# Four of each eight tokens' gated first one-hots made on GpSimd with scalar operands, the other four compared on VectorE

## The reference

```python
q = (xb @ w_q).reshape(PEER_BLOCK, PEER_HEADS, 2, PEER_QDIM // 2)
s = jnp.einsum('thpd,hpkd->thpk', q, subkeys)
s1, i1 = lax.top_k(s[:, :, 0], PEER_TOPK)
s2, i2 = lax.top_k(s[:, :, 1], PEER_TOPK)
...
sc, pos = lax.top_k(cand, PEER_TOPK)
idx = jnp.take_along_axis(cidx, pos, axis=-1)
g = jax.nn.softmax(sc, axis=-1)
act = jax.nn.gelu(jnp.einsum('thkd,td->thk', u[idx], xb))
return jnp.einsum('thk,thkd->td', g * act, v[idx])
```

## Time and profile before

| what | value |
|---|---|
| device time, 3 runs | 3705.79, 3709.24, 3708.85 us; median 3708.85 us |
| span of the profiled execution, first to last instruction | 3700.4 us; no separate total is given for that execution |
| PE, DVE, ACT, POOL busy | 96%, 72%, 54%, 4% of the span |
| gate phases, about | 1084 to 1181, 1970 to 2061, 3252 to 3338 us |
| POOL multiplies of the gate phase | 96, 102 us in all |

### The profile page before, as it was taken

How to read it: one execution, slowest core, us unless ns; L and a number is a source line. 1 busy time by engine, 2 the same in 40 slices (tenths; PEclk the granted TensorE clock), 3 DMA queues, 4 the chain that set the end, 5 groups by cost and what they waited for, 6 DMA issues and landing times.

```text
span 3700.4 us, 61292 instructions
## 1 busy us (share of the span) xinstructions
PE 3558.4 (96%) x22710; PEld 3113.8 (84%) x22710; DVE 2666.9 (72%) x5607; ACT 2003.8 (54%) x3922; POOL 139.6 (4%) x134
## 2 busy tenths in 40 slices
PE   7999999999998999999999999999899999979999
PEld 5877787888887899999998888888698888878888
DVE  5447733699868688888767776774765899686666
ACT  3345522566668555555557544434454666684444
POOL 0002000000012000000002000000100000030000
PEclk9999999999999999999999999999999999999999
DMA  5213222455645566566655566633044566605665
GB/s 206 82 67 138 94 97 83 144 183 182 186 151 159 167 187 184 185 186 184 187 184 152 161 186 198 195 119 111 9 164 136 176 187 182 187 29 165 188 190 172
DMA packets 142313, 568.38 MB, mean 154 GB/s; under 512 B 15920, under 2 KB 17456, under 8 KB 130352
## 3 DMA queue, kind: packets, MB, share of 16 engines
q1 hardware_dynamic: 142128, 566.16, 49.0%
HBM read 565.05 MB, written 1.05 MB: 153 GB/s over the span
## 4 chain that ended last, share of the span: by engine, by line
PE 82%; DVE 12%; ACT 3%; issue 2%; DMA 1%; POOL 1%; SPq 0%; DVEq 0%; POOLq 0%; ACTq 0%
PE ps L584 52%; PE ps L1081 13%; PE ps L1099 10%; PE ps L1083 6%; DVE low L1835 3%; DVE arena L1835 3%; ACT arena L1283 2%; DMA ring<-wmod_in 1%; POOL arena L2619 1%; DVE hot_found L1835 1%; DVE arena L2387 1%; DVE arena L2378 1%; DVE ring_low L1835 0%; DVE arena L2380 0%; DVE arena L2375 0%
## 5 line engine op out<-in xcount | busy, mean ns | idle before, releaser
L1283 ACT ACTIVATE high<-ring 128x512 fp32r<-128x512 f32 x1632 | 1028.4, 632 | 1014.7 <-PE ps L584 502.2
L1835 DVE TENSOR_TENSOR low<-ring,high 128x512 fp32r<-128x512 f32 x1632 | 1078.1, 690 | 290.4 <-ACT high L1283 279.4
L584 PE MATMUL ps<-h_pair,high 128*128 128x512 f32 x3456 | 1236.7, 398 | 17.6 <-DVE h_pair L1835 10.3
L584 PE MATMUL ps<-h_pair,low 128*128 128x256 f32 x3456 | 979.7, 283 | 0.0
L584 PEld LDWEIGHTS ps<-h_pair,high 128*128 128x128 f32 x3456 | 653.6, 189 | 171.1 <-issue 11.9
L1081 PE MATMUL ps<-wt,high 128*128 128x512 f32 x2016 | 706.3, 397 | 5.7 <-DVE low L1835 5.7
L584 PEld LDWEIGHTS ps<-h_pair,low 128*128 128x128 f32 x3456 | 655.0, 190 | 0.0
L1083 PE MATMUL ps<-wt,low 128*128 128x256 f32 x2016 | 562.4, 279 | 0.0
L1283 ACT ACTIVATE arena<-ps 128x256 f32<-128x256 f32 (+2 forms) x659 | 274.8, 427 | 382.3 <-PE ps L584 334.0
L1081 PEld LDWEIGHTS ps<-wt,high 128*128 128x128 f32 x2016 | 379.1, 188 | 97.2 <-issue 3.0
L584 PE MATMUL ps<-arena 128*128 128x128 f32 (+7 forms) x2536 | 355.1, 311 | 56.5 <-ACT arena L1283 44.2
(11 more groups left out here) (202 smaller groups left out, 4296.5 us busy)
## 6 DMA issues: line engine op xcount, KB each, us to landing
ring<-u_in SPq DMA_DIRECT2D x384, 512.0 KB, 3.6
ring<-v_in SPq DMA_DIRECT2D x384, 512.0 KB, 3.6
ring<-win_in SPq DMA_DIRECT2D x54, 1024.0 KB, 4.9
ring<-wmod_in SPq DMA_DIRECT2D x24, 1024.0 KB, 5.0
ring<-wq_in SPq DMA_DIRECT2D x48, 512.0 KB, 3.6
ring<-wmod_in SPq DMA_DIRECT2D x48, 512.0 KB, 3.7
ring<-wbr_in SPq DMA_DIRECT2D x16, 768.0 KB, 4.3
ring<-wout_in SPq DMA_DIRECT2D x8, 1024.0 KB, 4.9
```

The lines of the kernel that those rows point to most:

```text
L584: return pe.matmul(o, l_, r, start=first, stop=last)
L1283: return act.activation(o, i_, f, **kw_)
L1835: return dve.tensor_tensor(o, a, b, op)
```

## The change

`route_copy` writes the first indices a second time, as float32, into `RT[:, 1]`. `one_hot1` compares only tokens 4 to 7 of each group, 512 columns, and no longer waits for POOL. `gate_hot1` reads the smaller buffer. POOL makes tokens 0 to 3 by itself, an instruction of 128 columns each: compare the row 0..127 (`iota`, float32) with the token's index, multiply by its gate, both given as one scalar for each partition. It no longer waits for `hot1_found`; its waits for `route_read` and `g_product` stay.

```diff
 act.wait_ge(*at("route", pp, t))
 fn(route1[:, t * P:(t + 1) * P], ps[6][:, 0:P], ACT.Copy)
+fn(RT[:, 1, t * P:(t + 1) * P], ps[6][:, 0:P], ACT.Copy)
 fn(route2[:, t * P:(t + 1) * P], ps[6][:, P:2 * P], ACT.Copy)
...
 i = fn(hot1[:, g % 2, j, :],
-       hot1_found[:, g % 2, j // 2, :].rearrange("p (a b) -> p a b", b=2)[:, :, j % 2],
+       hot1_found[:, g % 2, j // 2 - GROUP // 4, :].rearrange("p (a b) -> p a b", b=2)[:, :, j % 2],
        ACT.Copy, scale=RT[:, 2, tk:tk + 1])
...
 if g >= 2:
     dve.wait_ge(*at("hot1", pp, g - 2))
-    dve.wait_ge(*at("ssd_xd", "hot1", pp, g - 2))
-tt(hot1_found[:, g % 2, :, :].rearrange("p a (k b) -> p a k b", b=2),
-   rep(iota_twice, GROUP // 2).rearrange("p a (k b) -> p a k b", b=2),
-   route1[:, g * GROUP:(g + 1) * GROUP].rearrange("p (a b) -> p a b", b=2).unsqueeze(2).broadcast_to(
-       [P, GROUP // 2, P, 2]), ALU.is_equal).then_inc(*inc("hot1_found", pp, g))
+tt(hot1_found[:, g % 2, 0:GROUP // 4, :].rearrange("p a (k b) -> p a k b", b=2),
+   rep(iota_twice, GROUP // 4).rearrange("p a (k b) -> p a k b", b=2),
+   route1[:, g * GROUP + GROUP // 2:(g + 1) * GROUP].rearrange("p (a b) -> p a b", b=2).unsqueeze(2
+       ).broadcast_to([P, GROUP // 4, P, 2]), ALU.is_equal).then_inc(*inc("hot1_found", pp, g))
...
 pool.wait_ge(*at("route_read", pp, 1))
 for g in range(GROUPS):
-    pool.wait_ge(*at("hot1_found", pp, g))
     if g >= 2:
         pool.wait_ge(*at("g_product", pp, g - 2))
-    mult(hot1[:, g % 2, 0:GROUP // 2, :].rearrange("p (a b) k -> p a b k", b=2),
-         hot1_found[:, g % 2, 0:GROUP // 4, :].rearrange("p a (k b) -> p a b k", b=2),
-         over(RT[:, 2, g * GROUP:g * GROUP + GROUP // 2].rearrange("p (a b) -> p a b", b=2), P)
-         ).then_inc(*inc("ssd_xd", "hot1", pp, g))
+    for tk in range(g * GROUP, g * GROUP + GROUP // 2):
+        i = pool.tensor_scalar(hot1[:, g % 2, tk % GROUP, :], iota, RT[:, 1, tk:tk + 1],
+                               RT[:, 2, tk:tk + 1], ALU.is_equal, ALU.mult)
+    i.then_inc(*inc("ssd_xd", "hot1", pp, g))
```

## The result

The changed kernel takes 3783.32 us (median of 4 runs, 3779.13 to 3789.71), the kernel before 3709.05 in the same comparison: +74 us, ratio 1.0201, 95% interval 1.0185 to 1.0218. The forecast of 3711 and its range up to 3733 were wrong; the slower rival, GpSimd as the bound, is what happened, beyond the part of it that the range took in. The profiled execution took 3779.13 us, with a span of 3777.3.

A forecast was written before the change was run, and what follows sets the result against it. Bound: TensorE in the middle gate phase, a 5.23 us loop without `one_hot1` in the last. Terms -0.8 + 3.1 = +2.3 us on the 3700.4 span, plus 8.5, gave 3711 us; 8-in-10 range 3703 to 3733.

The forecast's parts named there:

- the slower rival: Gate phases: GpSimd becomes the bound once four instructions exceed 2.6 us; 3721 us, 3827 at the ceiling; chance 0.29.
- What bounds the kernel: Gate phases: TensorE bounds the middle one, a loop without `one_hot1` the last; in the first, three engines take turns.
- The loop of 5.23 us: Last gate phase, two groups: products, `gate_mult`, `one_hot2`, ScalarE's `hot2`, then products again; 2.06 + 1.14 + 0.72 + 1.31.
- GpSimd's place in the chain: Last phase: the chain names GpSimd before `one_hot2`; called a tie with `gate_mult`, multiply ending at 3285.14 against 3285.21.
- Shorter `one_hot1`: VectorE, 96 comparisons cut from 1024 to 512 columns: 0.41 us each, mostly hidden; together -0.8 us, bounds 0 and -3.
- GpSimd: 4 `tensor_scalar` of 128 columns: GpSimd, each group: four instructions replace one multiply of 512; 0.36 us each, 1.44 a group, covered in all phases.
- The bound that a group can bear: Each gate group: GpSimd may take 2.8 us on latency and no more than 2.6 us on throughput.
- Contention: GpSimd's longer work reaches 0.4 us into `one_hot2` in the loop: 0.17 us each round, +3.1 us; bounds 0 and 6.5.
- The lock: Third rival: VectorE and GpSimd shut each other out fully; `one_hot2` waits out the instruction it meets; 3714.6 us; chance 0.13.
- Removed waits: VectorE's wait for GpSimd and GpSimd's for `hot1_found` go: long over or slack only, 0.
- `route_copy`: A fourth copy on ScalarE amid the chunks, 6 times 0.29 us, hidden under TensorE: 0, or 1.7 us if unhidden.
- keys: SP's held-back load of the keys waits for ScalarE's last group anyway: 0.

The follow-up runs named there:

- two instructions: Changed kernel, but from the third group on GpSimd makes two tokens of each group and the other two aren't made: 3709.51 us, ratio 0.9991 to the kernel before.
- three tokens: Changed kernel, but GpSimd makes three of its four tokens in each group and the fourth isn't made: 3718.03 us, ratio 1.0020 to the kernel before.

## Why the prediction was wrong

*What bounds the kernel.* Right. The loop of 5.23 us without `one_hot1` stood unchanged at 5.23 when the comparison was shortened and GpSimd had little to do, and the shorter comparison alone gave 0.9997. That GpSimd's place in the chain was a tie was right too.

*Shorter `one_hot1`.* Right: 0.41 forecast, 0.418 measured. The -0.8 us is too small to be told from nothing, and nothing is what was measured.

***GpSimd: 4 `tensor_scalar` of 128 columns.*** **This step failed.** "I take the fill as what is paid per instruction and a quarter of the old multiply for the columns: 0.10 + 0.26 = 0.36": alone it is 0.79 (0.77 from start to start), in place 0.90, so that a group took 3.6 us where 1.44 was forecast and 2.6 could be borne. Both halves were too small. The fill of one column reads nothing, and stood for an instruction with three operands: 0.10 for 0.36. And I took the columns of a comparison and a multiply to cost what those of a plain multiply do: 0.26 for 0.43. With the two bounds at 0.4 and 4.2 us the value sat near the floor, on the argument that only the part per instruction was a guess; it was the part that was paid four times. The bounds themselves held: 3.6 lies between them, near the ceiling.

*The bound that a group can bear*, 2.6 us, was right: two instructions, 1.57 us in the row above, hid; three, 2.84, showed at once.

*Contention.* Right that the two would meet, wrong in who pays and how. +3.1 us was charged to `one_hot2` in the loop; with two instructions a group `one_hot2` overlapped GpSimd and the loop stayed at 5.23. GpSimd paid, 0.50 us a group. Under a forecast of slack that looked harmless; with GpSimd as the bound it was 15 of the last phase's 31 us.

*The lock.* "0.77 us of overlap cost GpSimd only 0.32, which is sharing": this misread. GpSimd's multiply starts at 1063.38 while a subtraction runs to 1063.83, and is 0.32 longer than its 1.04; the second subtraction starts under it and itself pays, 0.18. Each time the one that began later was the longer for it; the first subtraction kept its 0.68. The runs show the same for the changed kernel: the instruction of GpSimd that begins under the comparisons ends 0.58 us after both, where alone it takes 0.79. That the two engines shut each other out in full was an assumption of the third rival, and no run shows it. What it had wrong is that `one_hot2` would wait out the whole instruction that it meets, where in the changed kernel it took 0.87 at most for 0.68, and that GpSimd would lose both comparisons in full: it lost 0.5 us of their 1.0, because one of its instructions was under way when they began.

*The slower rival* had the right bound, and its own formula with 3.6 us put in gives 30 x (1.0 + 0.8 + 0.4) = 66 us; 76 were measured, the rest in the first phase, whose groups I had priced at 3.2 us where they took 89.2 / 30 = 3.0. Its chance of 0.29 was split so that most lay near the lower end, and the row that it needed did not exist. The upper end of the range was also added up wrongly. At 0.75 an instruction, with 0.5 for the comparisons, a group is 3.5 us, and the rival's formula gives 30 x (0.88 + 0.67 + 0.3) = 56 us, 3764. The 3733 that was given is a group of 3.1 us, or 0.66 an instruction. Against the rival stood that two of the three operands are one column wide. With constants in their place the instruction took 0.15 us less (0.64 for 0.79; 0.17 from start to start); what in the two takes it, no run shows.

*Removed waits, `route_copy`, keys.* No effect found in the trace; not tried singly.

## What to carry to other kernels

Where an instruction replaces another on an engine that has never run it, count how many times the unknown part is paid before choosing a value between far bounds; four small instructions are not one large one cut up (4 x 0.79 us here, where one of 512 columns took 2.07). Look at single instructions before explaining a mean: 0.90 us here is 0.77 three times and 1.3 once. When the bounds are 0.4 and 4.2 and the slack ends at 2.6, the range must reach the far end. Before an engine is relieved, write out the loop that closes on itself: the busiest engine of the last phase (67 of 74 us) was not its bound, and moving one line of order gave what 26 us less work did not.

## What the runs showed of the hardware

- GpSimd's `tensor_scalar` with `is_equal` and `mult` and two scalars per partition takes 0.36 us per instruction and 3.35 ns a column (a line through the medians of 32 and 512 columns, 0.466 and 2.072 us, which meets those of 64 and 128), 0.79 us for 128. Its `tensor_tensor` multiply, two tensor inputs, does 512 columns in 1.04 us, half of the 2.07 of one `tensor_scalar` of that width, and 768 in 1.47.
- Undisturbed, `tensor_scalar` of 128 columns took 0.45 us with mult and add, and 0.79 with `is_equal` and `mult` and the same scalars. Which of the two operations makes the difference was not measured.
- A comparison of VectorE with both operands in SBUF holds up a `tensor_scalar` of GpSimd that begins under it: in the last phase it mostly took 1.30 or 1.31 us in the changed kernel and 1.13 or 1.48 with three tokens, for 0.79, and ended 0.58 after the comparisons. One already under way kept its 0.79 (30 of 30 in the last phase). GpSimd holds up VectorE in turn: a comparison that began 0.19 us into a `tensor_scalar` took 0.79 for 0.68, one begun 0.30 into it 0.68, and beside a `tensor_tensor` of 768 columns some took 0.82, the longest 0.99.
